# A recurrent mixer's sample part on TensorE: own products in a fourth column group, new state in four row groups

## The reference

```python
# q, k, v, f of the new tokens; S0 is the cached 128x128 state of the sequence and head
G = cumsum(log_f)                                  # over the 4 tokens
o_inter = (q * exp(G)) @ S0                        # "state product"
A[t, s] = sum_d q[t, d] * exp(G[t] - G[s]) * k[s, d]   # s <= t: "own products"
o_intra = A @ v
S_new = S0 * exp(G_last) + (k * exp(G_last - G)).T @ v   # "new state", an output
o = rms_norm(o_inter + o_intra) * silu(gate)
```

## Time and profile before

| | |
|---|---|
| median of 3 runs | 2613.02 us (2607.78 to 2615.09) |
| the profiled execution | 2616.4 us, its span 2614.8 us |
| PE busy | 2576.7 us, 99% |
| DVE, ACT, POOL busy | 57%, 39%, 13% |
| mean granted TensorE clock | 0.992 of 2.4 GHz |
| HBM traffic | 162 GB/s over the span |

### The profile page before, as it was taken

How to read it: one execution, slowest core, us unless ns; L and a number is a source line. 1 busy time by engine, 2 the same in 40 slices (tenths; PEclk the granted TensorE clock), 3 DMA queues, 4 the chain that set the end, 5 groups by cost and what they waited for, 6 DMA issues and landing times.

```text
span 2614.8 us, 51520 instructions
## 1 busy us (share of the span) xinstructions
PE 2576.7 (99%) x19424; PEld 2536.5 (97%) x19424; DVE 1484.4 (57%) x2054; ACT 1015.0 (39%) x1409; POOL 344.1 (13%) x285
## 2 busy tenths in 40 slices
PE   8999999999999999999999999999999999999997
PEld 8999999999999999999999999999999999999997
DVE  5467787555554455555555776875555444555555
ACT  5344554433333333333333535543333333333333
POOL 2011113111110011111100111131111000111111
PEclk9999999999999999999999999999999999999998
DMA  6445444544455544544454444444444545444543
GB/s 224 154 139 170 149 141 145 172 163 163 160 169 161 167 155 166 171 161 167 160 161 156 166 147 141 141 161 161 160 162 167 177 153 173 161 163 160 169 161 124
DMA packets 115724, 419.97 MB, mean 161 GB/s; under 512 B 13376, under 2 KB 14656, under 8 KB 115584
## 3 DMA queue, kind: packets, MB, share of 16 engines
q1 hardware_dynamic: 109152, 397.72, 45.8%
q0 software_dynamic: 3472, 14.04, 1.5%
q10 hardware_dynamic: 3024, 7.16, 0.7%
HBM read 411.06 MB, written 11.87 MB: 162 GB/s over the span
## 4 chain that ended last, share of the span: by engine, by line
PE 96%; DVE 2%; POOL 1%; ACT 1%; issue 0%; DMA 0%; DVEq 0%; SPq 0%; ACTq 0%; POOLq 0%
PE gp L1424 31%; PE gp L1426 30%; PE gp L1425 30%; PE mb L1468 1%; PE mb L1579 1%; PE mb L1600 0%; PE mb L1592 0%; POOL acc L1352 0%; PE mb L1477 0%; PE mb L1567 0%; PE mb L1538 0%; DVE rstd L724 0%; PE mb L1634 0%; DVE wlo L699 0%; DMA raw<-wstream 0%
## 5 line engine op out<-in xcount | busy, mean ns | idle before, releaser
L1424 PE MATMUL gp<-xh,whi 128*128 128x288 f32 x4096 | 1228.2, 300 | 12.9 <-DVE xl L1123 9.8
L1425 PE MATMUL gp<-xl,whi 128*128 128x288 f32 x4096 | 1211.9, 296 | 0.0
L1426 PE MATMUL gp<-xh,wlo 128*128 128x288 f32 x4096 | 1208.0, 295 | 0.0
L699 DVE TENSOR_TENSOR wlo<-raw,whi 128x1024 fp32r<-128x1024 f32 x754 | 971.1, 1322 | 345.6 <-ACT whi L410 342.0
L410 ACT ACTIVATE whi<-raw 128x1024 fp32r<-128x1024 f32 x754 | 769.0, 1052 | 578.6 <-PE gp L1426 539.7
L1424 PEld LDWEIGHTS gp<-xh,whi 128*128 128x128 f32 x4096 | 771.5, 188 | 25.1 <-issue 24.1
L1426 PEld LDWEIGHTS gp<-xh,wlo 128*128 128x128 f32 x4096 | 774.5, 189 | 0.0
L1425 PEld LDWEIGHTS gp<-xl,whi 128*128 128x128 f32 x4096 | 772.6, 189 | 0.9
L1424 PE MATMUL gp<-fh,whi 128*128 128x288 f32 x1408 | 416.7, 296 | 0.0
L1425 PE MATMUL gp<-fl,whi 128*128 128x288 f32 x1408 | 415.4, 295 | 0.0
L1426 PE MATMUL gp<-fh,wlo 128*128 128x288 f32 x1408 | 414.0, 294 | 0.0
(11 more groups left out here) (249 smaller groups left out, 1868.1 us busy)
## 6 DMA issues: line engine op xcount, KB each, us to landing
raw<-wstream SPq DMA_DIRECT2D x754, 512.0 KB, 4.2
s<-s_cache POOLq DMA_DIRECT2D x8, 512.0 KB, 9.8
hs_out<-s ACTq DMA_DIRECT2D x8, 512.0 KB, 2.8
caches_out<-caches POOLq DMA_DIRECT2D x8, 496.0 KB, 8.0
x<-x_in ACTq DMA_DIRECT2D x4, 576.0 KB, 8.7
y_out<-x SPq DMA_DIRECT2D x4, 576.0 KB, 2.8
kct<-kt_cache POOLq DMA_DIRECT2D x4, 512.0 KB, 6.5
vct<-v_cache POOLq DMA_DIRECT2D x4, 512.0 KB, 7.2
```

What stands on the lines that cost most here:

```text
L699: v.tensor_tensor(wlo[slot][:], raw[slot][:], whi[slot][:].bitcast(F32), ALU.subtract).then_inc(lo_ready, 1)
L1424: t.matmul(out, w_hi, mv_hi, start=first, stop=False)
L1425: t.matmul(out, w_hi, mv_lo, start=False, stop=False)
L1426: mm = t.matmul(out, w_lo, mv_hi, start=False, stop=last)
```

## The change

- `own`, `vst`, `vks`, `vm`, `ks4` get four copies of the 32 sample rows instead of three or two; `own` needs no zeroing, and the starting semaphore counts one less.
- **Own products** leave their place behind L1477 and go between the state products, into rows 96 to 127 of `mb[1]`, a column group of their own. The state products use three groups of rows of `mb[0]` (b mod 3). DVE masks the own products into rows 96 to 127 of `sel`, after `X` and before the next head's `opening`, instead of between `near(1)` and `level(3)`. `opening` waits for the last head's `X` instead of `L7`.
- **Output**: `xs` rows 96 to 127 take `v` (a new ACT copy of 32x128 from the transposed `v`), rows 0 to 95 the state products, so that one product `xs` by `sel` gives the samples' output; the product of `vks` and `ATs` goes.
- **New state**: four products of contraction 32, 256 columns each, in four banks, instead of two of 512. They wait for `xs` and for the masked own products as well.
- **Additions**: DVE adds sequences 0 and 1 after `ss` and the other six when ACT has copied `s2`, both ahead of the output's gating; `out` on PE waits for the first, `norm` for the second. ACT copies `s2` after `ss` instead of after `hp`. POOL's `vm` product has 128x256 elements instead of 96x512.

```diff
-TWICE = 96
+COPIES = P // SAMP
+NEW_STATE = ((0, 0), (1, 0), (2, 0), (3, P))
...
# scalar, hgrn
-                a.activation(vks[:, 0, :], mb[2][0:TWICE, 256:384], ACT.Copy).then_inc(ha.sem, ha.step("vt"))
+                a.activation(xs[P - SAMP:P, :], mb[2][P - SAMP:P, 256:384], ACT.Copy)
+                a.activation(vks[:, 0, :], mb[2][:, 256:384], ACT.Copy).then_inc(ha.sem, ha.step("vt"))
...
-                a.activation(xs[:], mb[0][:, 384:512], ACT.Copy).then_inc(ha.sem, ha.step("X"))
+                a.activation(xs[0:P - SAMP, :], mb[0][0:P - SAMP, 384:512], ACT.Copy).then_inc(ha.sem, ha.step("X"))
                 yield
                 a.wait_ge(h_store, T * 32 + 32)
-                a.wait_ge(ht.sem, ht.at(T, "hp"))
+                a.wait_ge(ht.sem, ht.at(T, "ss"))
...
# vector, opening
-                v.wait_ge(ht.sem, ht.last(T, "L7"))
+                v.wait_ge(ht.sem, ht.last(T, "X"))
...
# vector, hgrn: the masking of the own products, from behind near(T, 1, 1) to behind near(T, 4, 1)
+                own_rows = slice(P - SAMP, P)
+                v.wait_ge(ht.sem, ht.at(T, "X"))
+                v.tensor_tensor(sel[own_rows, :].rearrange("p (i r) -> p i r", r=2),
+                                strided(mb[1][own_rows, :], 256 + SAMP, (2, SAMP // 2), (SAMP + 1, 2)),
+                                const(C_HM)[own_rows, own_rows].rearrange("p (i r) -> p i r", r=2), ALU.mult
                                 ).then_inc(hv.sem, hv.step("bs"))
...
+                v.copy_predicated(sel[own_rows, :].rearrange("p (b j) -> p b j", j=4)[:, :, 2:4],
...
                 if not last:
                     opening(T + 1, h + 1)
                 yield
...
+                def new_state(name, groups):
+                    v.wait_ge(ht.sem, ht.at(T, "ss"))
+                    for i in groups:
+                        bank, at_ = NEW_STATE[i]
+                        for j in range(2):
+                            b = 2 * i + j
+                            m = v.scalar_tensor_tensor(s0[:, b, :], s0[:, b, :],
+                                                       lev_t(2)[:, SEQ // 4 + b:SEQ // 4 + b + 1],
+                                                       mb[bank][:, at_ + j * P:at_ + (j + 1) * P], ALU.mult, ALU.add)
                     m.then_inc(hv.sem, hv.step(name))
-                sample_state(0, "ssa", 1)
+                new_state("ssa", (0,))
+                v.wait_ge(ha.sem, ha.at(T, "hp"))
+                new_state("ssb", (1, 2, 3))
...
-                sample_state(1, "ssb", 2)
...
# tensor, hgrn
-                t.wait_ge(hv.sem, hv.last(T, "ssa"))
-                for r in range(2):
-                    t.matmul(mb[1][0:SAMP, 256 + (r + 1) * SAMP:256 + (r + 2) * SAMP], lev_k(r)[:, SEQ:TOK], q[:, SEQ:TOK],
-                             start=True, stop=True)
-                t.matmul(mb[1][0:SAMP, 256:256 + SAMP], lev_k(1)[:, SEQ:TOK], lev_q(1)[:, SEQ:TOK], start=True, stop=True)
+                t.wait_ge(hv.sem, hv.last(T, "ssb"))
...
-                for b in range(DEC_BATCH):
-                    rows = slice(32 * (b % 4), 32 * (b % 4) + 32)
-                    mm = t.matmul(mb[0][rows, 384:512], qz[:, b, :], s0[:, b, :], start=(b < 4), stop=(b >= 4))
+                t.wait_ge(hv.sem, hv.at(T, "e4"))
+                own_rows = slice(P - SAMP, P)
+                for i in range(3):
+                    for b in range(3 * i, min(3 * i + 3, DEC_BATCH)):
+                        rows = slice(SAMP * (b % 3), SAMP * (b % 3 + 1))
+                        mm = t.matmul(mb[0][rows, 384:512], qz[:, b, :], s0[:, b, :], start=(b < 3), stop=(b + 3 >= DEC_BATCH))
+                    left, right = ((0, q), (1, q), (1, lev_q(1)))[i]
+                    at_ = 256 + ((1, 2, 0)[i]) * SAMP
+                    mm = t.matmul(mb[1][own_rows, at_:at_ + SAMP], lev_k(left)[:, SEQ:TOK], right[:, SEQ:TOK],
+                                  start=True, stop=True)
                 mm.then_inc(ht.sem, ht.step("X"))
...
+                t.wait_ge(ha.sem, ha.at(T, "X"))
+                t.wait_ge(hv.sem, hv.at(T, "e1s"))
-                for i in range(2):
-                    rows = slice(64 * i, 64 * i + SAMP)
-                    mm = t.matmul(mb[1 + i][:], vks[rows, 1, :], vm[rows].rearrange("p b e -> p (b e)"),
+                for i, (bank, at_) in enumerate(NEW_STATE):
+                    rows = slice(SAMP * i, SAMP * (i + 1))
+                    mm = t.matmul(mb[bank][:, at_:at_ + 2 * P], vks[rows, 1, :], vm[rows].rearrange("p b e -> p (b e)"),
                                   start=True, stop=True)
                 mm.then_inc(ht.sem, ht.step("ss"))
                 yield
-                t.wait_ge(ha.sem, ha.at(T, "X"))
+                t.wait_ge(hv.sem, hv.at(T, "ssa"))
...
-                t.matmul(mb[0][:, SEQ:TOK], vks[0:SAMP, 0, :], ATs[:], start=True, stop=False)
-                mm = t.matmul(mb[0][:, SEQ:TOK], xs[:], sel[:], start=False, stop=True)
+                mm = t.matmul(mb[0][:, SEQ:TOK], xs[:], sel[:], start=True, stop=True)
                 mm.then_inc(ht.sem, ht.step("out"))
                 yield
                 t.wait_ge(ha.sem, ha.at(T, "osq"))
-                t.wait_ge(ha.sem, ha.at(T, "hp"))
+                t.wait_ge(hv.sem, hv.at(T, "ssb"))
```

More of the change, by code:

```diff
@@ L159, in build @@
         sel = sb("sel", [P, SAMP])
-        own = sb("own", [TWICE, 4])
+        own = sb("own", [P, DEC_BATCH // COPIES])
         qz = sb("qz", [P, DEC_BATCH, SAMP])
@@ L219, in build @@
         AT = sub(t, "AT", [P, 3, P])
-        ATs = sub(t, "ATs", [SAMP, SAMP])
-        vst = sub(t, "vst", [P, SEQ + TWICE])
+        vst = sub(t, "vst", [P, SEQ + P])
         vk = sub(t, "vk", [P, 4, P])
-        vks = sub(t, "vks", [TWICE, 2, P])
+        vks = sub(t, "vks", [P, 2, P])
         t[0] = max(t[0], temp[0] + 14496)
@@ L226, in build @@
         s0 = sub(t, "s0", [P, DEC_BATCH, P])
-        vm = sub(t, "vm", [TWICE, 4, P])
+        vm = sub(t, "vm", [P, DEC_BATCH // COPIES, P])
         xs = sub(t, "xs", [P, P])
-        ks3 = sub(t, "ks3", [P, 3, SAMP])
+        ks4 = sub(t, "ks4", [P, COPIES, SAMP])
         osb = sub(t, "osb", [P, TOK])
@@ L462, in hgrn @@
                 a.activation(vk[:, 2:4, :], two(mb[3][:, 0:256]), ACT.Copy)
-                a.activation(vks[:, 1, :], mb[3][0:TWICE, 256:384], ACT.Copy).then_inc(ha.sem, ha.step("kt"))
+                a.activation(vks[:, 1, :], mb[3][:, 256:384], ACT.Copy).then_inc(ha.sem, ha.step("kt"))
                 a.wait_ge(ht.sem, ht.at(T, "X"))
-                a.activation(xs[:], mb[0][:, 384:512], ACT.Copy).then_inc(ha.sem, ha.step("X"))
+                a.activation(xs[0:P - SAMP, :], mb[0][0:P - SAMP, 384:512], ACT.Copy).then_inc(ha.sem, ha.step("X"))
                 yield
                 a.wait_ge(h_store, T * 32 + 32)
-                a.wait_ge(ht.sem, ht.at(T, "hp"))
+                a.wait_ge(ht.sem, ht.at(T, "ss"))
                 apart(a)
@@ L605, in ffn_part @@
                     pair(i)
-            a.wait_ge(ones_set, 5)
+            a.wait_ge(ones_set, 4)
             a.activation(one_col[:, 1:2], eps[:], ACT.Copy)
@@ L748, in half_masks @@
                     v.tensor_reduce(sel[:], ident.rearrange("p (g t) -> p t g", t=SAMP), AX.X, ALU.add)
-                    for i in range(2):
-                        m = v.tensor_copy(own[64 * i:64 * i + SAMP, :], const(C_VM)[0:SAMP, 4 * i:4 * i + 4])
+                    for i in range(COPIES):
+                        m = v.tensor_copy(own[SAMP * i:SAMP * (i + 1), :], const(C_VM)[0:SAMP, 2 * i:2 * i + 2])
                 m.then_inc(masks_made, 1)
@@ L865, in hgrn @@
                 yield
+                own_rows = slice(P - SAMP, P)
[3 more added lines that the diff above has]
+                                const(C_HM)[own_rows, own_rows].rearrange("p (i r) -> p i r", r=2), ALU.mult
+                                ).then_inc(hv.sem, hv.step("bs"))
+                v.wait_ge(hv.sem, hv.at(T, "bs"))
+                apart(v)
+                apart(v)
+                v.copy_predicated(sel[own_rows, :].rearrange("p (b j) -> p b j", j=4)[:, :, 2:4],
+                                  half_mask[1][own_rows, P // 4 - DEC_BATCH:].bitcast(mybir.dt.uint32).unsqueeze(2)
+                                  .to_broadcast([SAMP, DEC_BATCH, 2]),
+                                  mb[1][own_rows, 256:256 + SAMP].rearrange("p (b j) -> p b j", j=4)[:, :, 2:4]
+                                  ).then_inc(hv.sem, hv.step("e1s"))
                 if not last:
@@ L1165, in _ @@
                 v.wait_ge(const_loaded, 16)
-                v.wait_ge(ones_set, 5)
+                v.wait_ge(ones_set, 4)
                 half_masks(l)
@@ L1241, in _ @@
             e.memset(eps[:], NORM_EPS).then_inc(ones_set, 1)
-            e.memset(own[:], 0.0).then_inc(ones_set, 1)
             e.memset(qz[:], 0.0).then_inc(ones_set, 1)
@@ L1282, in hgrn @@
                 apart(e)
```

(8 more changed lines are left out.)

27 lines of the change are left out of this document (7 added, 20 removed).

## The result

The changed kernel takes 2598.07 us (median of 5 runs, 2597.48 to 2599.77) against 2613.02 us (five runs, 2607.78 to 2615.09): ratio 0.9949, 95% interval 0.9937 to 0.9962. That is 14.95 us less, where 8.3 were forecast. Put down to the eight heads alone it would be 1.87 us a head instead of 1.04; it isn't theirs alone, as the profiles show.

What follows compares the result with a forecast made beforehand. PE's own instructions were taken as the bound; -0.39 - 0.45 + 0.22 - 0.42 = -1.04 us a head, times 8 = -8.3 us, from the median 2613.0 to 2604.7 us, range 2601 to 2611.

Steps and rivals of the forecast that it cites:

- part 1: Own products leave their place behind L1477, and the 32-column partition is no longer entered there: -0.39 us a head.
- part 2: Samples' output as one stacked product; L1546 and both changes of partition go: -0.45 us a head.
- rival on the clock: Stretches at half clock: one lost or added, 1.7 us, 2603.0 or 2606.4 us; chance 0.11 shared with unseen gains.
- part 3: State products in three column groups, two rounds more, own products free in the fourth: +0.22 us a head.
- Part 4: New state as four products side by side in four row groups, 0.64 us for 1.06: -0.42 us a head.
- Part 5: PE's new waits on masks, additions and copies: none bites, costed at nothing; `out` in time by 0.87 us.
- slow row groups: New state: four row groups no faster than two, -5.0 us in all, 2608.0 us; chance 0.13, partly slower included.
- broken rounds: State block: own products break the rounds of four, 2607.8 us, or 2614.9 fully serial; chance 0.13.
- late DVE: First additions late, PE stands before `out`: costs from 0.87 us of delay, 2616.6 us with one more `wlo`; chance 0.05.

Runs made afterwards that it cites:

- own products back: Changed kernel with the three own products back behind the head's first products, state products still in three column groups: 2602.8 us, ratio 0.9972 to the kernel before.
- two products of 512 columns: Changed kernel with the new state again as two products of 512 columns in two row groups: 2602.5 us, ratio 0.9970 to the kernel before.

## Why the prediction was wrong

The sign and the mechanism were right, the median fell under the range (2601 to 2611) by 2.9 us, and 14.95 us came where 8.3 were forecast. Of the 6.6 us between them:

- **1.9 us: the terms for leaving a partition were too small** (parts 1 and 2). In part 1 I counted 0.39 us a head and the block gave 0.49 to 0.50: the products behind the own products took 0.47 us before, 0.37 now, because the first one after the change of partition has its load in the open. I counted the gap on the way in and nothing on the way back, though the trace had it (164.08 to 164.55). In part 2 it is 0.53 for 0.45: I left two loads of 0.11 for the stacked product, 0.22 us, and 0.14 are left, since without a change of partition the first load lies beside L1557. Undone one by one, the parts give back 3.9 and 4.1 us less the clock's part, where 3.1 and 3.6 were counted. The state block cost 0.20 for 0.22, the new state gave 0.42 to 0.43 for 0.42.
- **About 3.6 us: the reference point.** I set the forecast against a median of 2613.0 us. The same kernel had 2609.2 to 2609.4 in 53 later runs and 2610.5 in 12 of its own. Its runs spread over 7 us, and its profiled execution, at 2616.4 us, stood above all of those shown. I put only a few microseconds for that spread into the range. My rival on the clock had one stretch in it, up or down; the profile held 27.3 us at half clock, worth 13.6 us in all.
- **About 1.2 us are left**, 11.4 us on the pooled medians (2609.4 and, for ten runs of the changed kernel, 2598.0) against 10.2 by the heads. The medians lie above the clock-free times by 6.3 us before and 5.2 after, and by 3 to 9 us in the other kernels with no order that I can see. Whether shorter heads change the mean number of stretches is open.

Point by point: **part 3** as forecast, own products free (own products back: 0.78 us with and without them). **Part 4** as forecast, 0.42 us. The 3.07 times that the Trainium skill gives for four row groups of 512 columns (TensorE: Matmul & The Clock Gate, "Measured speedup vs the span model") would have made it 0.29 us as I applied it, to the streaming alone. The trace, with 256 columns, has 4 x 0.43 us of streaming in a block of 0.64 us: 4 times without the way in and out, 2.7 with it. So applied to the streaming the figure is off here; as a ratio for the whole block it isn't refuted. **Part 5**: no wait, as forecast, with less to spare for `out` (0.37, not 0.87), since the opening starts 0.35 us behind the second mask. Of the **rivals**, the one of slow row groups is ruled out by the two products of 512 columns, the one of broken rounds by the order that made no difference; the late DVE is real as a mechanism but begins at 0.37 us and needs an insertion to show; the clock goes with about half of the error. The Trainium skill's rule, TensorE: Matmul & The Clock Gate, "The mechanism", that all matmuls start and end in the program's order, is at odds with the starts of the own products placed last; the increment of `X`, which waits for the products ahead, agrees with it.

## What to carry to other kernels

When an engine is full, count its stream start to start, and take a price from the middle of a run of like instructions. At a block's edges look at the weight loads too: the first load is covered by the product ahead, unless the array's partition changes in between, and then it shows on top of the gap. Small products that forced such a change cost about 0.5 us a head here (0.50 the own products, 0.53 the second product of the output); an unused column group made the first free, and stacking into a neighbour's rows did away with the second. And before a difference of half a per cent is reckoned from one profile, look at how much of that execution ran at half clock, and set sums against the time without it.

## What the runs showed of the hardware

- Column groups run side by side and out of the program's order: own products placed behind eight state products started 0.25 us after the block's start, 0.53 us before its end, and all six records before the last four state records. The semaphore on the last of them changed only when the state products ahead were done.
- A change of the array's partition puts the next weight load in the open: L1547's first load started with its product at 188.89, while without the change L1558's started 0.11 us ahead of its product at 185.15.
- Four row groups of 32, 256 columns each, in four PSUM banks, took 0.64 us with way in and out, of which, by two records of 0.215, 0.43 is the streaming time of one.
- Identical executions differ in the stretches at 1.2 GHz: 27.3 and 10.2 us of them in two profiles of one kernel. They come behind the sample attention's small products and where PE stands for the first opening of a layer, and each of 3.4 us costs 1.7. By the granted clock of whole runs of the kernel before: 2615.5 us on average at 0.992 (9 runs), 2610.4 at 0.994 (15), 2608.8 at 0.995 (21), 2607.7 at 0.996 (8).
